# GpSimd's key products of the dilated caches begin in the projection stage: queries turned and copied early, five key buffers, another order of loads and sums

## What is computed

```python
h = rmsnorm(x)
qa, ka, va, qb, kb, vb, qc, gates = split(h @ w_in)   # partial rotary on qa, ka, qb, kb
# A: window 128; C: 256 memory tokens
# B: query group g sees keys at distances 0, d, 2d, ... window
DIL_PAIRS = ((128, 1), (512, 4), (2048, 16))
s = einsum('bqhgd,bqkhd->bhgqk', q, k_ext[:, idx]) * HEAD_DIM ** -0.5
# softmax; the three groups are combined by their denominators
x = x + merge(oa, ob, oc, gates) @ w_out
x = x + moe(rmsnorm(x))      # top 4 of 32 experts, every expert's weights are read
```

## Time and profile before

| | us |
|---|---|
| median of three runs | 1320.06 |
| the profiled execution | 1318.04 |
| its span | 1316.2 |
| PE busy | 1215.7 (92%) |
| DVE, ACT, POOL busy | 419.9, 234.3, 81.1 |
| DMA moved | 502.37 MB, mean 382 GB/s |

### The profile page before, as it was taken

How to read it: one execution, slowest core, us unless ns; L and a number is a source line. 1 busy time by engine, 2 the same in 40 slices (tenths; PEclk the granted TensorE clock), 3 DMA queues, 4 the chain that set the end, 5 groups by cost and what they waited for, 6 DMA issues and landing times.

```text
span 1316.2 us, 14753 instructions
## 1 busy us (share of the span) xinstructions
PE 1215.7 (92%) x6122; PEld 515.3 (39%) x6122; DVE 419.9 (32%) x913; ACT 234.3 (18%) x459; POOL 81.1 (6%) x88
## 2 busy tenths in 40 slices
PE   9999589499999999999999999898999999899996
PEld 4456356377653333333333333333333333233332
DVE  2244466122553142231322313222221313122233
ACT  3212323123021112011210202101011102101012
POOL 0001533600020000000000000000000000000000
PEclk9999799799999999999999999999999999999998
DMA  8998885968979999999999999999999999999994
GB/s 309 383 356 307 258 299 180 333 184 289 418 278 390 400 428 429 428 427 427 429 428 428 426 429 428 428 427 426 429 428 428 429 428 427 427 428 429 428 427 187
DMA packets 74264, 502.37 MB, mean 382 GB/s; under 512 B 6992, under 2 KB 31184, under 8 KB 48576
## 3 DMA queue, kind: packets, MB, share of 16 engines
q1 hardware_dynamic: 72672, 496.84, 93.2%
q0 software_dynamic: 1520, 4.52, 1.1%
HBM read 498.42 MB, written 37.03 MB: 407 GB/s over the span
## 4 chain that ended last, share of the span: by engine, by line
PE 60%; DMA 34%; DVE 3%; issue 1%; SPq 1%; POOL 1%; ACT 1%; DVEq 0%; ACTq 0%; POOLq 0%
PE ps L1777 19%; DMA ring<-in_w_gate_up 16%; PE ps L1816 10%; DMA tail<-in_w_gate_up 6%; DMA late<-in_w_gate_up 6%; PE ps L1166 5%; PE ps L1250 5%; PE ps L1733 4%; PE ps L1677 3%; PE ps L1527 2%; DMA cq<-in_cache_dil_k 2%; PE ps L1540 2%; DMA ring<-in_cache_mem_k 1%; PE ps L1228 1%; PE ps L1794 1%
## 5 line engine op out<-in xcount | busy, mean ns | idle before, releaser
L1777 PE MATMUL ps<-ring,cq 128*64 128x512 f32 x1232 | 280.5, 597 | 22.1 <-DMA ring<-in_w_gate_up 22.1
L1777 PEld LDWEIGHTS ps<-ring,cq 128*64 128x64 f32 x1232 | 84.0, 136 | 193.2 <-issue 144.2
L1816 PE MATMUL ps<-ring,cq 128*64 128x512 f32 x592 | 134.3, 595 | 0.7 <-issue 0.7
L1250 PE MATMUL ps<-arena,ring 128*128 128x288 f32 x384 | 103.5, 416 | 1.8 <-ACT ring L909 1.8
L1050 ACT ACTIVATE cq<-ps 128x512 f32<-128x512 f32 x32 | 19.1, 597 | 451.2 <-PE ps L1794 451.2
L2301 DVE TENSOR_REDUCE tail<-ps 128x1 f32<-128x288 f32 x15 | 6.9, 457 | 290.1 <-PE ps L1709 290.1
L1250 PEld LDWEIGHTS ps<-arena,ring 128*128 128x128 f32 x384 | 70.5, 192 | 25.9 <-issue 5.4
L1166 PE MATMUL ps<-ring,arena 128*128 128x512 f32 (+3 forms) x240 | 72.3, 555 | 1.0 <-DMA ring<-in_w_in 1.0
L1816 PEld LDWEIGHTS ps<-ring,cq 128*64 128x64 f32 x592 | 41.0, 137 | 73.3 <-issue 69.8
L2329 DVE TENSOR_TENSOR x_tok<-x_tok,ps 64x512 f32<-64x512 f32 (+2 forms) x51 | 43.9, 860 | 68.0 <-PE ps L1733 62.3
L1677 PE MATMUL ps<-h_tok,cq 128*64 128x512 f32 x248 | 60.0, 605 | 0.0
(11 more groups left out here) (392 smaller groups left out, 1321.6 us busy)
## 6 DMA issues: line engine op xcount, KB each, us to landing
ring<-in_w_gate_up SPq DMA_DIRECT2D x77, 2048.0 KB, 42.6
ring<-in_w_down SPq DMA_DIRECT2D x37, 2048.0 KB, 43.9
tail<-in_w_gate_up SPq DMA_DIRECT2D x13, 2048.0 KB, 40.9
late<-in_w_gate_up SPq DMA_DIRECT2D x12, 2048.0 KB, 41.7
cq<-in_w_gate_up SPq DMA_DIRECT2D x12, 2048.0 KB, 42.3
arena<-in_w_gate_up SPq DMA_DIRECT2D x12, 2048.0 KB, 42.7
ring<-in_w_in SPq DMA_DIRECT2D x9, 2048.0 KB, 10.9
out_dil_k_s<-in_cache_dil_k SPq DMA_DIRECT2D x8, 2044.0 KB
```

The costliest lines, as they stand in the source:

```text
L1250: ins = pe.matmul(bank(gate_bank(m))[:, 0:TT], wblk[(6 + m // 4) % 2][:, k, (m % 4) * P:(m % 4 + 1) * P], hT_v[:, k, :], start=(k == 0), s ...
L1777: ins = pe.matmul(bank(gu0 + u)[64 * h:64 * h + 64, :], xTe[:, k % 4, (k // 4) * 64:(k // 4) * 64 + 64], pair_buf[slot][:, a:a + 512], sta ...
L1816: ins = pe.matmul(bank(7 if last else 5)[64 * h:64 * h + 64, :], aT[:, kk % 4, (kk // 4) * 64:(kk // 4) * 64 + 64], pair_buf[slot][:, a:a ...
```

## The change

- The key buffers are five: three in `aux` (a part of the weight ring that is unused in the projection stage), used for sequences 0 to 5, and the two old ones for 6 and 7. `qwin`, `osel`, `kTs2`, `k_dot` and the last `q_rep` move to other places to make room; the zeros are written to the new `qwin`.
- The rotary of the decode tokens' eight heads of groups 1 and 2 is done directly behind the sum of block n = 2 (`q_ready`), and left out of the later rotary of tile 2. ACT issues the DMA that writes them to HBM, and the eight that read them back, behind its eviction of (n, t) = (3, 0), where it waits for the first.
- The loads of keys 0 to 2 stand behind `load_wblk(4)`, 3 to 5 behind `load_wblk(6)` (each waits for a sum: 1, 2, 3), 6 and 7 behind `load_wblk(7)` (they wait for `tr_evicted`).
- Sums 0, 1 and 2 stand in DVE's list ahead of the rotary of tile 0, behind that of tile 1 and behind that of tile 2, all ahead of the evictions of the turns. Sums 3 to 7 stand behind units 0 to 4.
- Dot keys 0 to 3 wait for six sums, 4 for all products; those of 5 to 7 now stand directly behind `load_wblk(11)`. Cache copies stand later: two each behind blocks 2 and 3, one each behind 5 and 7, two behind `store_new_kv`, two behind block 9, three behind block 10, then 1, 1 and the last one where it was (before: eleven by block 7, then one at a time).

```diff
-        kTs2 = [aux[:, 896 * i:896 * (i + 1)] for i in (0, 1)]
+        kTs2 = [aux[:, 1024 + 896 * i:1024 + 896 * (i + 1)] for i in (0, 1)]
...
-        qwin = aux[:, 4768:7072].rearrange("p (c n) -> p c n", c=8)
-        qwin_v = aux[:, 4768:7072].rearrange("p (c b n) -> p c b n", c=8, n=36)
...
-        osel = aux[:, 7072:7840].rearrange("p (m g t) -> p m g t", m=6, g=4)
+        osel = aux[:, 7168:7936].rearrange("p (m g t) -> p m g t", m=6, g=4)
...
+        qw_area = gate_area[:, 18 * TT:26 * TT]
+        qwin = qw_area.rearrange("p (c n) -> p c n", c=8)
+        qwin_v = qw_area.rearrange("p (c b n) -> p c b n", c=8, n=36)
...
-        k_dil = [cring[:, 2048 * i:2048 * (i + 1)] for i in (0, 1)]
-        k_dot = [gate_area[:, 20 * TT + 896 * i:20 * TT + 896 * (i + 1)] for i in (0, 1)] + \
-            [aux[:, 1792 + 896 * i:1792 + 896 * (i + 1)] for i in range(3)]
+        k_dil = [aux[:, 1024 + 2048 * i:3072 + 2048 * i] for i in (0, 1, 2, 0, 1, 2)] + \
+            [cring[:, 2048 * i:2048 * (i + 1)] for i in (0, 1)]
+        k_dot = [aux[:, 2816 + 896 * i:2816 + 896 * (i + 1)] for i in range(4)] + [tail[:, 2432:3328]]
...
-        q_rep = [tail[:, 512 * b:512 * (b + 1)] for b in range(7)] + [aux[:, 1024:1536]]
+        q_rep = [tail[:, 512 * b:512 * (b + 1)] for b in range(7)] + [gate_area[:, 7680:8192]]
...
-        val_in = [S["cache0_in"], S["cache1_in"]] + [sem(f"val{k}_in") for k in range(2, NVS)]
+        val_in = [S[f"cache{k}_in"] for k in range(NVS)]
...
-        KEYS_IN = 16 * 7 * (NB_S // 2)
+        KEYS_IN = 16 * 7
+
+        def keys_in(b):
+
+            return val_in[b - 6 if b >= 6 else 2 + b % 3], KEYS_IN * (b // 3 + 1 if b < 6 else 1)
...
-            COPIES_BEHIND = (0, 0, 2, 2, 2, 1, 1, 3, 1, 1, 1)
+            COPIES_BEHIND = (0, 0, 2, 2, 0)
...
-                s, sm = k_dil[b % 2], S[f"cache{b % 2}_in"]
-                if b >= 2:
-                    sp.wait_ge(S["k_sum"], b - 1)
+                s, (sm, _) = k_dil[b], keys_in(b)
+                if b >= 6:
+                    sp.wait_ge(S["tr_evicted"], TR_H + TR_Q)
+                elif b >= 3:
+                    sp.wait_ge(S["k_sum"], b - 2)
                 src = d["cache_dil_k"][0, b].rearrange("r h n -> r (h n)")
                 for r in range(4):
...
                     sp.wait_ge(S["kt_done"], 2 * (b - len(k_dot) + 1))
+                elif b == 4:
+                    sp.wait_ge(S["k_mul"], NB_S)
+                else:
+                    sp.wait_ge(S["k_sum"], 6)
                 s = k_dot[n]
                 sp.dma_start(s[:, 0:256], d["cache_dil_k"][0, b].rearrange("r h n -> r (h n)")[1920:2048]).then_inc(dot_in[n], 16)
...
-            for i in range(1, 8):
+            for i in range(1, 5):
                 load_wblk(i)
                 for _ in range(COPIES_BEHIND[i]):
                     copy_cache()
-            sp.wait_ge(S["tr_evicted"], TR_H + TR_Q)
-            sp.wait_ge(S["q_out"], 16)
-            load_dilated_keys(0)
-            load_dilated_keys(1)
-            load_wblk(8)
-            store_new_kv()
-            load_dot_keys(0)
-            load_dilated_keys(2)
-            load_dot_keys(1)
-            load_dilated_keys(3)
-            load_wblk(9)
+            for b in range(3):
+                load_dilated_keys(b)
+            load_wblk(5)
             copy_cache()
-            load_dilated_keys(4)
-            load_dot_keys(2)
-            load_dilated_keys(5)
-            load_dot_keys(3)
+            load_wblk(6)
+            for b in range(3, 6):
+                load_dilated_keys(b)
+            load_wblk(7)
             copy_cache()
             load_dilated_keys(6)
             load_dilated_keys(7)
-            load_wblk(10)
+            load_wblk(8)
+            store_new_kv()
+            copy_cache()
+            copy_cache()
+            for b in range(4):
+                load_dot_keys(b)
+            load_wblk(9)
+            copy_cache()
+            copy_cache()
             load_dot_keys(4)
             load_values(0)
             load_values(1)
             load_values(2)
+            load_wblk(10)
+            copy_cache()
+            copy_cache()
+            copy_cache()
             load_wblk(11)
+            for b in range(5, NB_S):
+                load_dot_keys(b)
             for x in "kv":
                 n = (LA - NQ_S) * 128
                 src = d[f"cache_swa_{x}"][0].rearrange("b r h n -> b (r h n)")[:, NQ_S * 128:]
@@ -634,8 +651,6 @@
                     .then_inc(S["copy_dma"], 16)
 
             copy_cache()
-            for b in range(5, NB_S):
-                load_dot_keys(b)
             copy_cache()
             load_values(3)
...
-            pool.memset(aux[:, 4768:7072], 0.0).then_inc(S["zeros"], 1)
+            pool.memset(qw_area, 0.0).then_inc(S["zeros"], 1)
...
-            pool.wait_ge(S["rope_done"], 5)
-            pool.dma_start(d["q_rows"], q_tok[0:NS, 2, 768:1280]).then_inc(S["q_out"], 16)
-            pool.wait_ge(S["q_out"], 16)
-            q_rows = d["q_rows"].rearrange("(b i) n -> i b n", i=NQ_S)
-            for i in range(NQ_S):
-                pool.dma_start(tail[i::NQ_S, 0:7 * 512].rearrange("p (b n) -> p b n", n=512),
-                               q_rows[i, 0:7].unsqueeze(0).to_broadcast([P // NQ_S, 7, 512])).then_inc(S["q_rep_in"], 16)
-                pool.dma_start(q_rep[7][i::NQ_S, :],
-                               q_rows[i, 7].unsqueeze(0).to_broadcast([P // NQ_S, 512])).then_inc(S["q_rep_in"], 16)
             pool.wait_ge(S["q_rep_in"], 16 * 2 * NQ_S)
 
             for b in range(NB_S):
 
-                pool.wait_ge(S[f"cache{b % 2}_in"], 16 * 7 * (b // 2 + 1))
-                k = k_dil[b % 2].rearrange("p (c n) -> p c n", n=256)
+                pool.wait_ge(*keys_in(b))
+                k = k_dil[b].rearrange("p (c n) -> p c n", n=256)
                 q4, q16 = q_rep[b][:, 0:256], q_rep[b][:, 256:512]
                 pool.tensor_tensor(k[:, 0, :], k[:, 1, :], q16, ALU.mult).then_inc(S["near_done"], 1)
...
@@ -884,6 +891,16 @@
                     else:
                         ins = act_e.activation(q[:, 1280:1536], pb[:, 0:256], ACT.Copy, scale=qs)
                     ins.then_inc(S["proj_evicted"], 1)
+                    if (n, t) == (3, 0):
+                        act_e.wait_ge(S["q_out"], 16)
+                        for i in range(NQ_S):
+                            act_e.dma_start(tail[i::NQ_S, 0:7 * 512].rearrange("p (b n) -> p b n", n=512),
+                                            q_rows[i, 0:7].unsqueeze(0).to_broadcast([P // NQ_S, 7, 512])).then_inc(S["q_rep_in"], 16)
+                            act_e.dma_start(q_rep[7][i::NQ_S, :],
+                                            q_rows[i, 7].unsqueeze(0).to_broadcast([P // NQ_S, 512])).then_inc(S["q_rep_in"], 16)
+                if n == 2:
+                    act_e.wait_ge(S["q_ready"], 1)
+                    act_e.dma_start(d["q_rows"], q_tok[0:NS, 2, 768:1280]).then_inc(S["q_out"], 16)
                 if n == 0:
...
-                pe.wait_ge(val_in[b % NVS], 16 * 9 * (b // NVS + 1) + (KEYS_IN if b % NVS < 2 else 0))
+                pe.wait_ge(val_in[b % NVS], 16 * 9 * (b // NVS + 1) + KEYS_IN * (1 if b % NVS < 2 else 2))
...
+
+            def rope(t, src, nh, name):
+
...
+                sbc = sin.unsqueeze(1).to_broadcast([r, nh, 8])
+                v.tensor_tensor(T[0], x1, cb, ALU.mult)
+                v.tensor_tensor(T[1], x2, sbc, ALU.mult)
+                v.tensor_tensor(T[2], x2, cb, ALU.mult)
+                link(v.tensor_tensor(T[3], x1, sbc, ALU.mult))
+                v.tensor_tensor(x1, T[0], T[1], ALU.subtract)
+                signal(v.tensor_tensor(x2, T[2], T[3], ALU.add), name)
+
+            def sum_keys(b):
+
+                v.wait_ge(S["k_mul"], b + 1)
+                v.tensor_reduce(sT[:, 32 * b:32 * b + 32], k_dil[b].rearrange("p (c n) -> p c n", n=HD), AX.X, ALU.add) \
+                    .then_inc(S["k_sum"], 1)
+
...
-            tmp = probs
+                if n == 2:
+                    v.wait_ge(S["proj_evicted"], 9)
+                    rope(2, q_tok[0:NS, 2, 768:1280], 8, "q_ready")
+
+
+            sum_keys(0)
+                r, nq = NTOK[t], 20 if t < 2 else 12
+                rope(t, q_tok[0:r, t, 0:nq * HD], nq, "rope_done")
+                rope(t, kv[0:r, t, 0:384], 6, "rope_done")
+                if t >= 1:
+                    sum_keys(t)
             for n in range(TR_Q):
                 evict_tr(TR_H + n, TR_H + n)
...
-            SUMS_BEHIND = (1, 2, 4, 5, 7, 8, 10, 11)
+            SUMS_BEHIND = (0, 1, 2, 3, 4)
             unit_stats(0)
             for u in range(NU):
                 if u + 1 < NU:
                     unit_stats(u + 1)
                 unit_norm(u)
                 if u in SUMS_BEHIND:
-                    sum_keys(SUMS_BEHIND.index(u))
+                    sum_keys(3 + SUMS_BEHIND.index(u))
```

30 lines of the change are left out of this document (10 added, 20 removed).

## The result

The changed kernel takes 1306.88 us (median of four runs, 1304.07 to 1311.08) against 1320.66 for the kernel before beside it (1318.82 to 1321.40): a ratio of 0.990, 95% interval 0.9871 to 0.993. That is a gain of 13.8 us where 27.6 was forecast, and it lies 1.9 us outside the range given (1279 to 1305).

The account below looks back on a forecast made before the run. The experts' half is bound by its weights, so gains come from starting it earlier by shortening the chain before 391.47 us: 39.0 - 8.0 - 1.4 - 2.0 = 27.6 us, giving 1292.4 us; range 1279 to 1305.

Parts of the forecast that it names:

- the units' gaps: TensorE idle times of 13.16 and 5.62 us in the attention units, released by DVE's norm; both were to go.
- 19.1 forecast: Units' stage, until the first turn of dot keys: 13.16 + 5.62 + 2.3 (slow matmuls) - 2.0 us gained.
- Products 6 and 7: GpSimd products beside the first units, holding DVE's small instructions: 2.0 us added, between 0 and 10.
- 8.0 + 1.4: Entry to the units: first turn's eviction 8.0 us later, then TensorE slow after its wait, 1.4 us.
- the 1.2 + 5.0 of the prediction: Rotary of tile 0: it meets the end of product 1 (about 1.2 us) and all of product 2 (5.0).
- the prediction's own rival of late queries: Queries land at 88 or later, sum 0 and everything behind it wait: 1300 to 1304 us; chance 0.17.
- Ahead of them are three copies and a block, issued in the units 20 us and more before: Loads ahead of dot keys 5 to 7, taken as issued early enough that all 17.95 us of wait go.
- Copies moved later: nothing, up to 5: Cache copies issued later move the same bytes in the first half: no cost, up to 5 us.
- the gap stays, 0.08: Dot keys' gap stays if copies and block 11 are still queued: up to 18 us return, 1310; chance 0.08.
- 17.95: TensorE's idle time ending at 258.22, waiting for sequence 5's memory keys; all of it was to go.
- the lock: A DVE instruction with two SBUF inputs waits for a whole GpSimd instruction; reckoned in the rotary and first units.
- an expected shift of 27: The first half was to shorten by 27 us, with the experts starting from about 364 instead of 391.47.

Follow-up runs that it names:

- the quiet rotary: Changed kernel with product 1 held behind the whole rotary, product 4 behind four units, sums, key buffers and block 9 reordered: 1306.34 us, ratio 0.9885.
- the last kernel but one above: The version with block 10 ahead of the values, with one cache copy issued behind values 2 instead of beside the experts' loads: 1288.10 us, ratio 0.9761.

## Why the prediction was wrong

**Right.** What bounds the kernel (the start of the experts, one to one), the units' gaps (13.16 and 5.62 are gone), and the mechanism of the added cost: small rotary instructions that wait for whole GpSimd instructions, shown by the run without products 0 to 3 and by the quiet rotary. The Trainium skill's rule (SBUF — State Buffer, section "Who interferes with whom") is that a DVE instruction with two SBUF inputs contends with a GpSimd instruction that reads SBUF, and a `tensor_reduce` never. The rows of the changed kernel agree: the sum takes 2.29 us beside a GpSimd product (88.82) and alone (109.00). Evictions from PSUM weren't held either: that at 122.06 takes 0.69 us beside product 4, as those of its size do elsewhere.

That the units' stage came out near its forecast (20.5 us gained, 19.1 forecast) is in part luck. Products 6 and 7 cost some 4 us there and not 2.0, and gaps and slow matmuls that the prediction hadn't counted made up for it: in the kernel before TensorE stood four more times for 0.2 to 0.9 us, and the sixteen gate matmuls at 156.78 took 5.17 us, 4.16 elsewhere.

**The entry, 5.1 us short** (8.0 + 1.4 became 14.5). The terms that were mis-sized: the contention was put at 7.5 and is 10.3 (8.8 - 2.6 for tile 0, the 1.2 + 5.0 of the prediction, and 6.7 - 2.6 for tile 1); product 3 was counted half, since I had its keys land at 97 and reckoned half of it onto the scaling and sum 1, but they landed at 103.19, with the rotary of tile 1, and 4.1 us of its 5.2 were paid. The queries were put at 80 and landed at 83.8, and DVE, first in its list with sum 0, stood 2.65 us; the prediction's own rival of late queries, in small. The eight issues on ACT took 6.9 us instead of 5, and the landing up to 8.0. The last 0.6 us are matmuls that ran slow behind the wait: 2.0 us and not 1.4.

**Dot keys, 9.0 us short.** The step that failed is the sentence "Ahead of them are three copies and a block, issued in the units 20 us and more before". The copies were issued 20.6 us before the dot keys, the block only 10.2 us, as it waits for its buffer; and 20 us aren't enough, for these 8.2 MB are some 26 us of work at 315 GB/s. I had checked in the list only which load stands ahead of which, not how many bytes are in flight in the stretch: the DMA share is 0.95 there. "Copies moved later: nothing, up to 5" was the same error: without the late copies the whole gap is gone, and with the three elsewhere too. In the prediction this was a rival (the gap stays, 0.08) that had been left out of the range. It came halfway: 8.9 of the 17.95 us were gained.

**The decode softmax, 4.3 us, not foreseen.** The prediction put nothing here: it looked for the lock where the change moved GpSimd's work and not where it moved DVE's. Everything downstream of a gain comes earlier, but a task on another engine whose time is set by loads (the bias splits) stays, and 15 us earlier the two overlap. It could have been read off: GpSimd's rows up to 264, DVE's softmax from 268, and an expected shift of 27.

**The range.** It was built from one deviation at a time. Here three middling ones came together, 18.4 us less 1.4, and nothing made them exclude each other, as the list of rivals with one chance each had it.

**Open.** Why the three issues of values on SP take 12.19 us (11.95 and 12.34 in the runs without products 0 to 3 and 6 and 7), and the same row in the quiet version 2.2, was not separated from the state of the queues; the order of loads differs by several entries. What this hold costs the changed kernel wasn't tried. What a copy costs beside the experts' loads is open too. From the mark to the end it took 908.2 to 908.5 us with one copy behind the first expert loads (the kernel before, the changed kernel), 908.10 with three (the last kernel but one above) and 911.7 to 912.7 with four (three kernels); the other runs with one copy or none there lie between 907.4 and 909.2. So the fourth cost about 4 us and the two before it nothing. Why there is room for three and not for four wasn't tried.

## What to carry to other kernels

A gain upstream is worth what the loads downstream let through, and they let it through where the issues ahead of them come forward with it: sum the bytes that are in flight between the gain and the next wait, not only the order of the list, and ask of each load on a full queue when it will be issued if everything in front of it is needed sooner. When one engine's work moves earlier, look at what then lies beside it on the engine that it can block, the unmoved tasks included. A product on GpSimd costs nothing beside DVE work that sums or reads PSUM, and most of its length beside chains of small two-input instructions (6.2 of 8.0 us and 4.1 of 5.2 here). Waits that keep them apart gave nothing alone; together with the splits behind the softmax and the loads in the order of need they were worth more here (20 us) than the whole change (14).

## What was unexpected in the hardware

- A `TENSOR_SCALAR` of 128x4 f32 in SBUF took 1.73 us beside a GpSimd product and 0.17 without, and one of 128x896 took 1.46 and 0.69: the wait is not for `TENSOR_TENSOR` alone, the only kind that the prediction reckoned with.
- In these rows the wait falls mostly on DVE's side: GpSimd's products grew from 1.79 to 1.89 us and from 2.47 to 2.65 for two, and its casts beside the softmax from 0.60 to at most 0.89, while DVE's instructions of 0.32 grew to between 0.75 and 1.93.
- An issue of a DMA on SP, 0.4 to 0.6 us, took 10.90 us with the DMA engines full (394 GB/s over these 10.90 us; 292 over the 13 us before), and one on ACT up to 1.22.
